# Second mixer of a three-mixer trunk: softmax steps interleaved, part of its output projection among the last head groups, one modulation block earlier

## The reference

```
shift, scale, gate = split(silu(c) @ ada_w + ada_b)          # 1024 -> 3 x 1024, for each of 4 sites, + 6 x 1024 later
h = rms_norm(x, g) * (1 + scale) + shift
x = x + gate * mixer_or_experts(h)
```

```
s = q @ k.T * 64**-0.5 ; s = where(valid, s, -inf)
m = max(max(s), sink) ; e = exp(s - m) ; p = e / (sum(e) + exp(sink - m))
y = (p @ v) @ w_out
```

## Time and profile before

| | |
|---|---|
| median of 3 runs | 1837.54 us (1837.54 to 1840.82) |
| the profiled execution | 1838.14 us, its span 1836.0 us |
| TensorE busy | 1381.9 us (75%), 11264 matmul records |
| VectorE, ScalarE busy | 432.3 us (24%), 232.2 us (13%) |
| moved by DMA | 638.01 MB, mean 348 GB/s |

### The profile page before, as it was taken

The page is one execution under the profiler, slowest core; times in us unless marked ns, Lnnn a source line. Parts: engine busy times, 40 slices in busy tenths (PEclk is TensorE's granted clock), DMA queues, the critical chain, the costliest instruction groups (busy, mean ns, idle before and its releaser), DMA issues.

```text
span 1836.0 us, 25701 instructions
## 1 busy us (share of the span) xinstructions
PE 1381.9 (75%) x11264; PEld 746.8 (41%) x11264; DVE 432.3 (24%) x969; ACT 232.2 (13%) x480; POOL 25.8 (1%) x46
## 2 busy tenths in 40 slices
PE   7998666666665698797666656656899884999996
PEld 4655332333332343444333323322355642555553
DVE  1664110122000115523000100000216644211112
ACT  2122000010000012412000000000213222100001
POOL 1000000000000000000000000000020000000000
PEclk9998787888988899888877787878899996999998
DMA  9978999999999979839999999999930312699995
GB/s 377 352 297 352 427 423 427 425 425 424 425 425 424 420 296 353 334 100 386 422 427 424 426 424 425 425 424 426 404 127 24 138 37 78 274 421 421 421 421 219
DMA packets 88427, 638.01 MB, mean 348 GB/s; under 512 B 8476, under 2 KB 8476, under 8 KB 42240
## 3 DMA queue, kind: packets, MB, share of 16 engines
q1 hardware_dynamic: 84656, 623.76, 82.6%
q0 software_dynamic: 3664, 12.64, 2.0%
HBM read 635.30 MB, written 1.96 MB: 347 GB/s over the span
## 4 chain that ended last, share of the span: by engine, by line
DMA 47%; PE 43%; DVE 6%; ACT 2%; issue 1%; SPq 0%; DVEq 0%; ACTq 0%
PE ps L1890 41%; DMA ring<-in_moe_w_up 29%; DMA ring<-in_moe_w_down 12%; DMA ring<-in_ada_w 4%; PE ps L1893 2%; ACT work L2253 2%; DMA ring<-in_fc_w_in 2%; DMA ring<-in_moe_w 1%; DVE tmp L2508 0%; DVE x L2510 0%; DVE work L684 0%; ACT tmp L2253 0%; ACT xn L2253 0%; SPq L287 0%; DVE work L2609 0%
## 5 line engine op out<-in xcount | busy, mean ns | idle before, releaser
L1890 PE MATMUL ps<-ring,work 128*32 128x256 f32 (+3 forms) x7760 | 780.3, 465 | 343.9 <-DMA ring<-in_moe_w_gate 153.2
L1890 PEld LDWEIGHTS ps<-ring,work 128*32 128x32 f32 (+2 forms) x7760 | 360.0, 132 | 740.6 <-issue 294.6
L2253 ACT ACTIVATE work<-ps 128x256 f32<-128x256 f32 (+3 forms) x188 | 89.2, 479 | 1227.6 <-PE ps L1890 1015.3
L2643 DVE TENSOR_TENSOR work<-work,ps 128x256 f32<-128x256 f32 x32 | 13.5, 422 | 628.5 <-ACT work L2253 628.5
L1890 PE MATMUL ps<-work 32*128 32x256 f32 (+6 forms) x1034 | 140.4, 460 | 15.5 <-ACT work L2253 13.7
L1890 PEld LDWEIGHTS ps<-work 32*128 32x128 f32 (+3 forms) x1034 | 85.6, 211 | 68.8 <-issue 47.1
L1890 PE MATMUL ps<-ring,hT 128*128 128x512 f32 (+1 forms) x224 | 90.5, 564 | 1.1 <-DVE tmp L1481 1.1
L1890 PE MATMUL ps<-ring,condT 128*32 128x512 f32 x576 | 74.7, 634 | 9.4 <-DMA ring<-in_ada_w 9.4
L1893 PE MATMUL ps<-const,work 128*128 128x128 f32 (+1 forms) x394 | 65.9, 298 | 18.5 <-ACT work L2253 8.5
L1890 PE MATMUL ps<-work,xn 128*128 128x128 f32 (+2 forms) x416 | 68.1, 315 | 7.0 <-DVE work L1709 6.8
L1890 PE MATMUL ps<-hT,ring 128*128 128x256 f32 x288 | 67.4, 395 | 4.8 <-DMA ring<-in_fc_w_in 3.1
(11 more groups left out here) (303 smaller groups left out, 664.9 us busy)
## 6 DMA issues: line engine op xcount, KB each, us to landing
ring<-in_moe_w_gate SPq DMA_DIRECT2D x64, 2048.0 KB, 17.0
ring<-in_moe_w_up SPq DMA_DIRECT2D x64, 2048.0 KB, 17.7
ring<-in_moe_w_down SPq DMA_DIRECT2D x128, 1024.0 KB, 15.9
ring<-in_moe_w SPq DMA_DIRECT2D x102, 1024.0 KB, 11.3
ring<-in_ada_w SPq DMA_DIRECT2D x72, 1024.0 KB, 14.6
ring<-in_w_in SPq DMA_DIRECT2D x10, 1024.0 KB, 17.0
ring<-in_fc_w_in SPq DMA_DIRECT2D x6, 1024.0 KB, 16.0
ring<-in_attn_w_qkv SPq DMA_DIRECT2D x6, 1024.0 KB, 20.4
```

The lines of the kernel that those rows point to most:

```text
L1890: return pe.matmul(out, lhsT, rhs, start=start, stop=stop, skip_group_check=True)
L2253: return nc.scalar.activation(out, in_, f, **kw)
L2643: v.tensor_tensor(hid, act, ps[:, 5, 0:SEQ], ALU.mult).then_inc(S("hid_ready"), 1)
```

## The change

In mixer 2: (a) VectorE takes mask and maximum of group g ahead of the probabilities of group g-1, ScalarE the exponentials of g ahead of the copy of g-1. (b) The pieces of blocks 12 to 15 are dealt to steps 0 to 5 (`ADA_IN_GROUP`), the columns to steps 1, 2, 4 and 6. (c) Token tile 0's output projection is cut into four units, run in steps 6, 7, 8 and behind the loop, in banks 2 and 3; therefore the scores of groups 4 to 7 all use banks 0 and 1 and wait for the mask of the group before. Tile 1 is projected after the gate row, in banks 0 and 1, and alone counts the four pieces as used. (d) VectorE updates tile 0 of x when `out_ps` says so.

In mixer 1: block 6 goes ahead in the stream, between output pieces 1 and 2, and on TensorE between the gate row and the wait for the Silu rows, in bank 5. Block 7 follows output piece 3 in the stream and stays where it was on TensorE. The amount of work of each engine is the same.

```diff
+P_OUT_1 = P_FC_FOURIER + 2 + 12
+P_ADA_6 = P_OUT_1 + 2
+P_FC_OUT = (P_OUT_1, P_OUT_1 + 1, P_ADA_6 + 4, P_ADA_6 + 5)
+P_ADA_7 = P_ADA_6 + 6
+P_MOE_A = P_ADA_7 + 4
...
+        ADA_IN_GROUP = {0: (12, range(4)), 1: (13, range(4)), 2: (14, range(2)), 3: (14, range(2, 4)),
+                        4: (15, range(2)), 5: (15, range(2, 4))}
+        COLUMNS_IN_GROUP = {1: 12, 2: 13, 4: 14, 6: 15}
...
+        def scores_bank(g):
+            return 2 * (g % 2) if g < NKV else 0
...
-                    pe.wait_ge(S("masked"), g - 1)
+                    pe.wait_ge(S("masked"), g - 1 if g <= NKV else g)
...
+            def out_unit(T, kp):
+                loaded(pe, P_ATT_OUT + kp)
+                w = slot(P_ATT_OUT + kp).rearrange("p (k f) -> p k f", k=2)
+                for kk in range(2):
+                    k = 2 * kp + kk
+                    for h in range(2):
+                        last = mm(ps[:, 2 - 2 * T + h, :], oT[:, k, P * T:P * T + P], w[:, kk, 512 * h:512 * h + 512],
+                                  k == 0, k == KD - 1)
+                return last
...
-                if g < 4:
-                    ada_block(12 + g)
+                if g in ADA_IN_GROUP:
+                    b, pieces = ADA_IN_GROUP[g]
+                    if pieces.start == 0:
+                        pe.wait_ge(S("mod_copied"), copied(b - 1))
+                    for kp in pieces:
+                        ada_piece(b, kp)
+                if g >= 6:
+                    pe.wait_ge(S("oT_ready"), NKV)
+                    out_unit(0, g - 6)
+            out_unit(0, 3).then_inc(S("out_ps"), 1)
             pe.wait_ge(S("oT_ready"), NG)
             pe.wait_ge(S("mod_copied"), copied(15))
             gate_row(2, 0)
-            project_out(P_ATT_OUT, oT)
+            pe.wait_ge(S("masked"), NG)
+            for kp in range(4):
+                out_unit(1, kp).then_inc(S("piece_used"), 1)
...
-            dve.wait_ge(S("piece_used"), P_ATT_OUT + 4)
-            update_x(lambda T: ps[:, 2 * T:2 * T + 2, :])
+            dve.wait_ge(S("out_ps"), 2)
+            update_x(lambda T: ps[:, 2 - 2 * T:4 - 2 * T, :], P_ATT_OUT + 4)
...
-            plain_pieces(P_FC_OUT, A["fc_w_out"][0])
+            out_piece(0)
+            out_piece(1)
+            ada_pieces(6)
+            out_piece(2)
+            out_piece(3)
+            ada_pieces(7)
...
                 gate_row(0, 0)
+                pe.wait_ge(S("aside_arg"), 1)
+                ada_block(6)
                 pe.wait_ge(S("yc_ready"), 4)
...
             def experts(n0, layer, k, site, late):
-                pe.wait_ge(S("gate_ready"), layer + 1)
-                ada_block(late)
+                if layer:
+                    pe.wait_ge(S("gate_ready"), 2)
+                    ada_block(late)
+                else:
+                    pe.wait_ge(S("row_copied"), late + 1)
```

More of the change, by code:

```diff
@@ L298, in ada_at @@
         def ada_at(g):
-            for first, n in ((16, P_TAIL_B), (9, P_ADA_2), (8, P_ADA_8), (6, P_TAIL_A), (3, P_FC_FOURIER + 2),
+            for first, n in ((16, P_TAIL_B), (9, P_ADA_2), (8, P_ADA_8), (7, P_ADA_7), (6, P_ADA_6), (3, P_FC_FOURIER + 2),
                              (2, P_ADA_1), (1, P_ADA + 5), (0, P_ADA)):
@@ L545, in scores @@
                         o = slice(HD * b, HD * b + HD)
-                        last = mm(ps[:, 2 * (g % 2) + b, SEQ * a_:SEQ * a_ + SEQ],
+                        last = mm(ps[:, scores_bank(g) + b, SEQ * a_:SEQ * a_ + SEQ],
                                   qT[o, 2 * kv + a_, P * T:P * T + P], kT2[o, kv, :], a_ == 0, True)
                 last.then_inc(S("scores_ps"), 1)
+            def out_unit(T, kp):
[7 more added lines that the diff above has]
+                return last
             scores(0)
@@ L612, in act_attention @@
                 if g:
+                    g1, T, kv = groups[g - 1]
+                    sc_.wait_ge(S("pT_ps"), g1 + 1)
+                    if g1:
+                        sc_.wait_ge(S("oT_ps"), g1)
+                    act_(pT.rearrange("p h k s -> p (h k s)"), ps[:, 4:6, :].rearrange("p b s -> p (b s)"), ACT.Copy)\
+                        .then_inc(S("pT_ready"), 1)
                     sc_.wait_ge(S("oT_ps"), g1 + 1)
@@ L616, in act_attention @@
                         .then_inc(S("oT_ready"), 1)
-                if g < 4:
-                    ada_rows(12 + g)
+                if g in ADA_IN_GROUP and ADA_IN_GROUP[g][1].stop == 4:
+                    ada_rows(ADA_IN_GROUP[g][0])
         TWO_PI_HI = 6.28125
@@ L677, in dve_attention @@
             for g in range(NG + 1):
+                if g < NG:
+                    _, T, kv = groups[g]
+                    st = sm_[:, g % 2]
+                    dve.wait_ge(S("scores_ps"), g + 1)
+                    if g >= 2:
+                        dve.wait_ge(S("pT_ps"), g - 1)
+                    then(dve, v.scalar_tensor_tensor(
+                        sc[:, g % 2], ps[:, scores_bank(g):scores_bank(g) + 2, :]
+                        .rearrange("p b (a s) -> p (b a) s", a=2), HD ** -0.5, window[:, T].unsqueeze(1).broadcast_to([P, REP, SEQ]),
+                        op0=ALU.mult, op1=ALU.add), "masked")
+                    link(v.reduce_max(st[:, 0:4], sc[:, g % 2], X))
+                    link(v.tensor_tensor(st[:, 0:4].rearrange("p (b a) -> p b a", a=2),
+                                         st[:, 0:4].rearrange("p (b a) -> p b a", a=2), sink[:, kv], ALU.max))
+                    link(v.tensor_scalar(st[:, 0:4], st[:, 0:4], -1.0, None, ALU.mult))
+                    then(dve, v.tensor_tensor(st[:, 8:12].rearrange("p (b a) -> p b a", a=2),
+                                              st[:, 0:4].rearrange("p (b a) -> p b a", a=2), sink[:, kv], ALU.add),
+                         "negmax_ready")
                 if g:
@@ L686, in dve_attention @@
                          "probs_ready")
[L687 to L704, removed]
-                if 0 < g < 5:
-                    columns_out(11 + g)
+                if g in COLUMNS_IN_GROUP:
+                    columns_out(COLUMNS_IN_GROUP[g])
             dve.wait_ge(S("mod_copied"), copied(15))
@@ L1793, in conv_piece, with out_piece @@
                 stream(P_FC_IN[kp], v[:, kp // 2, 2 * (kp % 2):2 * (kp % 2) + 2, HALF:HALF + D])
+            def out_piece(kp):
+                stream(P_FC_OUT[kp], rows_of(A["fc_w_out"][0])[:, 2 * kp:2 * kp + 2, :])
             sp.dma_start(x[:, :, :], A["x"].rearrange("(t p) f -> p t f", p=P)).then_inc(S("x_loaded"), 16)
@@ L1825, in experts @@
                             load(sp, n, down[:, 0, kp])
-            for g in range(6, 8):
-                ada_pieces(g)
             experts(P_MOE_A, 0)
@@ L2132, in experts @@
                 last.then_inc(S("affT_ps"), 1)
+                if layer == 0:
+                    pe.wait_ge(S("gate_ready"), 1)
                 ada_block(late + 1)
@@ L2303, in norm @@
                     table_for(ACT.Exp)
-                    ada_rows(late)
+                    if k == 3:
+                        ada_rows(late)
                 else:
```

33 lines of the change are left out of this document (11 added, 22 removed).

## The result

The changed kernel takes 1816.66 us in the median of 4 runs (1810.99 to 1819.45), against 1837.54 for the kernel before in the same comparison: ratio 0.9882, 95% interval 0.9852 to 0.9912. By the ratio that is 21.7 us less, between 16 and 27. The forecast of 1815 lies 1.7 us under the median. The profiled execution took 1810.99 us (span 1808.9).

The account below looks back on a forecast made before the run. The prediction took the one weight stream through a ring of eight 1 MB places to set the expert stages' pace, with idle time at both mixers. 5.5 + 17.1 = 22.6 us off 1838.14 gave 1815; eight in ten, 1808 to 1829.

Parts of the forecast that it names:

- Part B: Second mixer: reordered softmax work and dealt-out pieces and output units save 17.1 us, bounds 19.1 and -13.
- part A: End of first mixer: block 6 ahead in the wait for the Silu rows saves 5.5 us, bounds 9.8 and -1.
- steps 3, 4, 5 and 6: Second mixer, bounded by TensorE: step 2 ends at 741.8, then steps 3 to 6 at 748.0, 755.3, 761.5 and 770.3.
- Tile 1's projection ends: End of second mixer: tile 1's four output units (13.8 us) end at 803.0, against 820.97 before, 18.0 us less.
- R3: Rival, second mixer: steps stay 7.05 us and only units 0 and 1 find room; total 1822, chance 0.13.
- The update under the matmuls: Behind the second mixer: tile 0's update lies under tile 1's matmuls; tile 1's x ready 2.5 us after projection, 5.1 before.
- block 16 gives part of this back: Behind the second mixer: block 16 (3.64 us) is only partly covered, so logits come 1.1 us sooner after the projection.
- The clock term: Second mixer: 2 us taken off the gain for a stretch of TensorE at half clock.
- 19.1 forecast for that case: Second mixer: upper bound of the gain, 19.1 us, if the clock does not fall.
- R1: Rival, second mixer: clock stays at 1.2 GHz from step 2 to the end of unit 3; total 1845, chance 0.05.
- The term for the stream: End of first mixer: block 6's pieces free ring places in the empty time, so the stream gains 6 us.
- the router logits end some 2.1 us earlier, I take 1.5: First experts: x and transposes move up, so router logits end some 2.1 us earlier, taken as 1.5.

Follow-up runs that it names:

- after_again: The changed kernel run once more, unedited, against the kernel before: 1815.73 us, ratio 0.9880.
- after: The changed kernel as first measured and profiled, against the kernel before: 1816.66 us median, ratio 0.9882; profiled execution 1810.99 us.
- b_only: The kernel before with only the mixer 2 changes, mixer 1 as before: 1817.19 us, ratio 0.9888 to the kernel before.
- block7_early: The changed kernel with block 7 moved between the two tiles' transposes of x at the first experts: 1814.98 us, ratio 0.9882 to the kernel before.
- block7_fill: block7_early plus four added matmuls, result unread, in the 3.91 us wait for the choice of tokens: 1812.64 us, ratio 0.9855 to the kernel before.
- filler: The changed kernel plus two matmul calls, result unread, ahead of tile 1's transposes in the first experts: 1815.19 us, ratio 0.9877 to the kernel before.
- pool_late: The changed kernel with GpSimd's filter and context loads (2.5 MB) held until the first expert pairs are used: 1824.53 us, ratio 0.9927 to the kernel before.
- softmax_only: The kernel before with only the new order on VectorE and ScalarE in mixer 2: 1830.99 us, ratio 0.9959 to the kernel before.
- split_gap: The changed kernel with mixer 2's step waits filled and block 7 halved between transposes and the wait for the choice: 1809.07 us, ratio 0.9847 to before.

## Why the prediction was right

**Part B, step by step, as forecast.** The forecast counted part B in the old time; part A brought mixer 2 forward by 5.07 us (644.33 to 639.26 for x after the first experts). With 5.07 added, the starts of steps 3, 4, 5 and 6 (scores at 736.72, 742.92, 750.22, 756.42) are 741.8, 748.0, 755.3 and 761.5, each the end that the forecast gave for the step before, to 0.1 us. Tile 1's projection ends at 783.87 + 13.90 = 797.77, so 802.8 for 803.0. This is because the durations came from rows of before at full clock, and nothing but TensorE's own work and its counted wait of 1.11 us for ScalarE bounds the new steps. R3 would have shown every step at 7.05 us or more (steps 3 and 5 took 6.2), and VectorE's wait of 2.31 us. Neither is there.

**The update under the matmuls.** x of tile 1 was expected 2.5 us after the projection, and its second operation starts at 799.13, 1.4 us after it (3.9 before), and ends 2.6 us after it. That block 16 gives part of this back was in the sum: M2 fell by 18.77 us, mixer 2 alone by 20.65.

**The clock term had the right size and came in some executions only.** The forecast took off 2 us for a stretch at half clock. In the profiled execution the granted clock is 1.00 in all of mixer 2 from 725 to 805, and M2 fell by 18.8 us (19.1 forecast for that case). In after_again the stretch is there: 0.66 in 735 to 740, with values of 2.02 us, and M2 fell by 16.5. Of seven executions with these steps, each of a different run, four held 1.00 from 725 to 790 (after, b_only, block7_early, block7_fill: M2 653.8 in the mean, 19.2 under before) and three had such a fall (after_again and filler one, pool_late two, 0.72 in 725 to 730 and 0.74 in 735 to 740; M2 655.9 in the mean, 17.1 under before). R1 did not occur in any. With waits of 1.11 us, one in 6.2 to 7.3 us, TensorE thus stayed at 2.4 GHz in four executions, and in three it was at 1.2 GHz for a few us. The rule that the prediction cites from the Trainium skill ("TensorE: Matmul & The Clock Gate", "A second HAM failure mode: psum-queue depth-cycling") would have it go back and forth; the traces bear out one fall or two, worth 2.1 us in M2, and none in four of the seven executions.

**Part A was mis-sized: 5.5 us predicted, 3.9 measured.** The interval of the 3.9 (0.9 to 7.0) holds the 5.5, so the medians alone don't show the error; the traces do. In the profiled execution stage 1 is 4.1 us shorter and x 1.0 us earlier, of which 0.3 was there at the gate row already (125.11 for 125.43): 4.8 in all. In the mean of six kernels with part A and block 7 in its old place stage 1 takes 494.8, in the three without part A (before, b_only, softmax_only) 497.9: 3.1, and 3.8 with the 0.7 in mixer 1. The term for the stream was right as far as it goes: in the profiled execution experts to x fell by 474.34 - 468.84 = 5.5 us (2.6 to 4.2 in the four kernels above the floor). It is cut off there, since it is the end of the backlog: before, TensorE waited 4.21 us for a piece of up at 179.59, behind the first expert matmuls, and after there is no such wait. The rows of before, which the earlier trace rows does not have:
```profile
151.22 3.73 PE L1890 MATMUL ps<-router_gain,hT 128*128 128x16 f32 x32
...
157.37 5.86 PE L1890 MATMUL ps<-ring,condT 128*32 128x512 f32 x32
...
165.64 3.81 PE L1890 MATMUL ps<-work,xn 128*128 128x128 f32 x32
...
179.59 3.29 PE L1890 MATMUL ps<-ring,work 128*32 128x256 f32 x32 [4.21 <-DMA ring<-in_moe_w_up]
```
The step that failed is "the router logits end some 2.1 us earlier, I take 1.5" and the start of the experts that followed from it. The logits ended 1.0 us earlier (153.96 for 151.22 + 3.73 = 154.95), 4.84 us long; block 7 took 6.27 us for 5.86 and the gather 5.44 for 3.81, both for the most part at 1.2 GHz (clock 0.50 in 156 to 160, 0.64 in 164 to 168). So the experts began 0.4 us later where I had them 1.5 us earlier. What I had not seen is that with the stream's backlog gone this chain, priced in the forecast as if it only triggered transfers, is itself the bound, or within 3 us of it. It was in the case for R2 ("the expert stage starts on TensorE's chain"), which I had dismissed as a whole because the stream has no pause after 144; after the change it has one (221 GB/s in 160 to 164).

A is 1.6 us too high, B about 1.2 us too low (18.3 in M2 for 17.1). They cancel, and that the sum is nearer than its terms is luck. The scatter of the rest of the program is larger than either error: 515.4 and 520.8 us in two profiles of one kernel. It lies in the third mixer, 202.2 and 207.8 us long up to its update of x, where the granted clock in the same stretch of work was 1.00 (after, 1373.44 to 1433.44) and 0.91 (after_again, 1377.40 to 1437.40). That the clock is the cause was not tested.

## What to carry to other kernels

Where a stream of weights has a ring in front of it, work moved into an idle stretch of the stream pays only until the ring is full at the next start. From there on, shorten the chain that leads to that start. Split its gain in two numbers, "mark to start" and "start to end", and see which one moves. When two engines alternate in a step, reordering one and refilling the other can be worth little apart (4.5 and 6.5 us in one profile each) and more together (18.3): the first makes room, and the second uses it. And fill a wait with work that has its own operands ready, piece by piece: the last 1.11 us per step were worth 6 us more.

## What the runs showed of the hardware

The 32 matmuls of the router's logits (128 x 16 results) took 3.72 to 6.99 us in 14 executions, and 4.84 and 6.99 in two of the same code (after, after_again): the granted clock fell from 1.00 to 0.50 at a varying moment within them or right behind them. They took 3.72 us in all three kernels in which the whole of block 7 ran between the transposes ahead of them, 4.34 with half of it (split_gap), and 5.79 behind two wide calls (filler). The same 3.73 came in the kernel before, with block 6 ahead of both transposes, but 4.04 and 4.98 in softmax_only and b_only, which have that same order. Block 7 behind them ran in part at the lower clock and took 4.9 to 6.3 us, against 3.64 for the same number of matmuls as block 6. In block7_fill the clock had fallen ahead of the added wide calls (0.50 in 156 to 160), came back only towards their end (0.52 in 160 to 162, 1.00 in 162 to 164), and fell again in the gather. During the first expert matmuls it is at 1.00 (172 to 176 in after). Why it falls in the narrow matmuls was not isolated.
